# Strassen weight sums of an encoder's gated MLP: from accumulating DMAs into on-chip buffers, just in time, to batches in a DRAM scratch

## The reference, cut to what matters

```python
def conv_ffn(h, p, buf):
    u = h @ p['w_ffn_up']
    a, v = u[..., :D_FF], u[..., D_FF:]
    T = a.shape[1]
    ext = jnp.concatenate([buf.astype(a.dtype), a], axis=1)
    w = p['ffn_conv_w']
    c = p['ffn_conv_b'] + sum(ext[:, j:j + T] * w[j] for j in range(CONV_W))
    out = (jax.nn.silu(c) * v) @ p['w_ffn_down']
    return out, ext[:, -(CONV_W - 1):]

def layer(x, pos, p, lb, kv_past, pe_past, past_pos, S0, conv_buf, is_prompt):
    h = rmsnorm(x, p['norm_mix_pre'])
    mix, kv_lat, k_pe, S_new = token_mixers(h, pos, p, lb, kv_past, pe_past, past_pos, S0, is_prompt)
    x = x + rmsnorm(mix, p['norm_mix_post'])
    h = rmsnorm(x, p['norm_ffn_pre'])
    f, buf = conv_ffn(h, p, conv_buf)
    x = x + rmsnorm(f, p['norm_ffn_post'])
    return x, kv_lat, k_pe, S_new, buf
```

## Time and profile before

| | |
|---|---|
| three runs | 1931.81, 1934.43, 1935.34 us |
| profiled execution, its own time | 1932.28 us |
| its span | 1930.5 us |
| TensorE busy | 1820.8 us, 94% |
| VectorE, ScalarE, GpSimd busy | 1267.4, 951.0, 229.5 us |
| DMA moved | 204.03 MB, mean 106 GB/s |
| mean granted TensorE clock | 0.979 |

### The profile page before, as it was taken

One profiled execution on the slowest core, in us unless ns is written; L12 is line 12 of the kernel. 1 busy time (PEld: TensorE's weight loads), 2 busy tenths in 40 slices (PEclk: granted clock), 3 DMA queues, 4 the chain that ended last, 5 costly groups with the idle time before them and its releaser, 6 DMA issues.

```text
span 1930.5 us, 31256 instructions
## 1 busy us (share of the span) xinstructions
PE 1820.8 (94%) x11636; PEld 1668.9 (86%) x11636; DVE 1267.4 (66%) x1973; ACT 951.0 (49%) x1593; POOL 229.5 (12%) x257
## 2 busy tenths in 40 slices
PE   8999999999899999898799999999998999999985
PEld 7999975698899999898799999657988999999984
DVE  5777875526765665677767778653377665756776
ACT  5444546436653443535654444653466343535355
POOL 0000034100112121111000000340001111111100
PEclk9999999999999999999999999999999999999997
DMA  4312131411565665565131122323125565556621
GB/s 178 91 57 68 62 95 52 134 54 40 130 159 142 153 142 141 138 156 140 44 106 46 57 68 72 88 74 96 60 76 145 142 151 143 141 149 166 140 71 60
DMA packets 98902, 204.03 MB, mean 106 GB/s; under 512 B 16864, under 2 KB 35680, under 8 KB 98728
## 3 DMA queue, kind: packets, MB, share of 16 engines
q1 hardware_dynamic: 63952, 144.39, 23.5%
q0 software_dynamic: 21888, 39.86, 12.6%
q10 hardware_dynamic: 12912, 17.78, 2.8%
HBM read 170.98 MB, written 8.65 MB: 93 GB/s over the span
## 4 chain that ended last, share of the span: by engine, by line
PE 56%; DVE 17%; DMA 13%; ACT 9%; issue 3%; DVEq 0%; POOL 0%; ACTq 0%; SPq 0%; POOLq 0%
PE G L795 34%; PE WA L795 11%; PE WB L795 8%; DVE wlo L2158 5%; DMA t<-in_wstream 4%; DMA wraw<-in_wstream 2%; ACT whi L1480 2%; DMA t<-wraw 2%; DVE tmp L2158 2%; DMA wff<-in_wstream 2%; DVE cc L2158 1%; DMA wraw<-t 1%; DMA wff<-t 1%; PE G L799 1%; DVE ax L2158 1%
## 5 line engine op out<-in xcount | busy, mean ns | idle before, releaser
L795 PE MATMUL G<-Hh,wlo 128*128 128x328 f32 x1384 | 452.4, 327 | 11.8 <-DVE Hl L2158 8.0
L795 PE MATMUL G<-Hh,whi 128*128 128x328 f32 x1384 | 436.0, 315 | 0.0
L795 PE MATMUL G<-Hl,whi 128*128 128x328 f32 x1384 | 434.6, 314 | 0.0
L795 PEld LDWEIGHTS G<-Hh,wlo 128*128 128x128 f32 x1384 | 263.2, 190 | 23.3 <-DVE Hl L2158 12.1
L795 PEld LDWEIGHTS G<-Hh,whi 128*128 128x128 f32 x1384 | 263.4, 190 | 2.4 <-issue 0.6
L795 PEld LDWEIGHTS G<-Hl,whi 128*128 128x128 f32 x1384 | 263.1, 190 | 0.0
L1480 ACT ACTIVATE whi<-wraw 128x1024 fp32r<-128x1024 f32 (+2 forms) x171 | 155.6, 910 | 187.0 <-PE G L795 114.7
L2158 DVE TENSOR_TENSOR wlo<-wraw,whi 128x1024 fp32r<-128x1024 f32 (+2 forms) x171 | 177.6, 1038 | 54.4 <-ACT whi L1480 41.8
L795 PE MATMUL G<-gh,wlo 128*128 128x328 f32 x424 | 134.3, 317 | 10.1 <-DVE tmp L2158 9.3
L795 PE MATMUL G<-Sh,wlo 128*128 128x328 f32 x304 | 100.9, 332 | 34.2 <-ACT R L1480 34.2
L795 PE MATMUL G<-gh,whi 128*128 128x328 f32 x424 | 132.9, 313 | 0.0
(11 more groups left out here) (327 smaller groups left out, 4142.9 us busy)
## 6 DMA issues: line engine op xcount, KB each, us to landing
wraw<-in_wstream SPq DMA_DIRECT2D x108, 512.0 KB, 3.5
wff<-in_wstream SPq DMA_DIRECT2D x40, 512.0 KB, 4.6
t<-in_wstream SPq DMA_DIRECT2D x76, 256.0 KB, 4.4
t<-in_wstream POOLq DMA_DIRECT2D x38, 256.0 KB, 6.5
ckT<-in_ckT SPq DMA_DIRECT2D x12, 512.0 KB, 3.4
wff<-in_wstream POOLq DMA_DIRECT2D x20, 256.0 KB, 4.1
t<-wff POOLq DMA_DIRECT2D x20, 256.0 KB, 3.9
wff<-t POOLq DMA_DIRECT2D x20, 256.0 KB, 3.5
```

What stands on the lines that cost most here:

```text
L795: return pe.matmul(out, lhsT, rhs, start=start, stop=stop, skip_group_check=True)
```

## The change

1. The sums T1 to T4 no longer lie in on-chip buffers. A new internal DRAM tensor `wsum` (2 layers x 19 chunks x 128 x 2048 floats, as [T2 | T3 | T1 | T4]) holds them. POOL makes them in five batches of 4, 4, 3, 4 and 4 chunks a layer: three plain copies from `wstream` (u into the places of T1 and T4, B22 into T2, B12 into T3), then accumulating DMAs for T1 and T3, then T2, then T4, each step when the one before has landed.
2. In each layer POOL makes batches 0 and 1 (EARLY = 2) before the heads' work, in layer 0 after `tile` reached 4, and batches 2 to 4 after `split_out`, before the MLP.
3. SP loads four pieces for each chunk in place of two and two copies: u; [T2 | T3] and [T1 | T4] from `wsum`, and the right half of v (B22) with 256 KB.
4. `t2` and `t3` (3 halves) go, `wff` gets a third buffer: five raw buffers in all in the MLP.
5. LATE and PAIRS change: T1 and T4 are split as a pair, B22 alone.
6. DVE makes `g_low` of chunk 2 before the sums of activations and not behind them.

The changed lines, cut to their core:

```diff
-RAW, SPL = 2, 3
+RAW, SPL, SLOTS = 2, 3, 5
...
-LATE = {B11: 1, B21: 0, T2: 1, T3: 0, T1: 0, T4: 1, B22: 0}
-PAIRS = (B11, T2, T4)
+LATE = {B11: 1, B21: 0, T2: 1, T3: 0, T1: 1, T4: 0, B22: 0}
+PAIRS = (B11, T2, T1)
+CHUNK_PIECES = 4
+BATCHES = [(NPL, 7), (7, FH), (FH, 14), (14, 18), (18, KF)]
+EARLY = 2
...
+    wsum = nc.dram_tensor("wsum", [DEPTH, NS, P, 2 * W_PIECE], F32, kind="Internal").ap()
...
         def raw_slot(p):
-            return p % 2 if p < P_UP + 2 * NPL else p % 4
+            return p % RAW if p < P_UP + 2 * NPL else (p - P_UP) % SLOTS
...
+                    return [[(s, 0, W_PIECE, 0)], [(None, 0, W_PIECE, 0)], [(None, W_PIECE, 2 * W_PIECE, 0)],
+                            [(s + 1, W_HALF, W_PIECE, 0)]][p - p0]
...
                 for c, p0 in P_CHUNK.items():
                     if p == p0 + 1:
-                        sum_parts(l, c)
+                        name, n = summing(l, next(b for b, (c0, c1) in enumerate(BATCHES) if c0 <= c < c1))
+                        sp.wait_ge(S(name), n + 112)
...
+            def start_sums(l, b):
+                (u, v, t), (name, n) = stored_parts(l, b), summing(l, b)
+                if n:
+                    pool.wait_ge(S(name), n)
+                pool.dma_start(t[:, :, W_PIECE:2 * W_PIECE], u).then_inc(S(name), 16)
+                pool.dma_start(t[:, :, to_t2], v[:, :, right]).then_inc(S(name), 16)
+                pool.dma_start(t[:, :, to_t3], v[:, :, left]).then_inc(S(name), 16)
+            def sum_t1_t3(l, b):
+                (u, v, t), (name, n) = stored_parts(l, b), summing(l, b)
+                pool.wait_ge(S(name), n + 48)
+                pool.dma_start(t[:, :, to_t1], v[:, :, left], accum_op=ALU.add).then_inc(S(name), 16)
+                pool.dma_start(t[:, :, to_t3], v[:, :, right], accum_op=ALU.add).then_inc(S(name), 16)
+            def sum_t2(l, b):
+                t, (name, n) = stored_parts(l, b)[2], summing(l, b)
+                pool.wait_ge(S(name), n + 80)
+                pool.dma_start(t[:, :, to_t2], t[:, :, to_t1], accum_op=ALU.add).then_inc(S(name), 16)
+            def sum_t4(l, b):
+                t, (name, n) = stored_parts(l, b)[2], summing(l, b)
+                pool.wait_ge(S(name), n + 96)
+                pool.dma_start(t[:, :, to_t4], t[:, :, to_t2], accum_op=ALU.add).then_inc(S(name), 16)
+            def weight_sums(l, b0, b1):
+                for b in range(b0, b1):
+                    start_sums(l, b)
+                for b in range(b0, b1):
+                    sum_t1_t3(l, b)
+                for b in range(b0, b1):
+                    sum_t2(l, b)
+                for b in range(b0, b1):
+                    sum_t4(l, b)
+            pool.wait_ge(S("tile"), 4)
             for l in range(DEPTH):
+                weight_sums(l, 0, EARLY)
                 for h in range(HG):
...
                 split_out(l, range(HG))
-                sum_t1(l, NPL)
-                sum_t2(l, NPL)
-                for c in range(NPL, KF):
...
+                weight_sums(l, EARLY, len(BATCHES))
...
                         lows(l, u0 - 1)
+                        g_low(last_c)
...
-                    g_low(last_c)
+                    if q:
+                        g_low(last_c)
```

More of the change, by code:

```diff
@@ L86 @@
         U_PROD[_c], P_CHUNK[_c] = _u, _p
-        _u, _p = _u + PRODUCTS, _p + 2
+        _u, _p = _u + PRODUCTS, _p + CHUNK_PIECES
     U_PASS[_q], P_PASS[_q] = _u, _p
@@ L225, in build @@
         cout = sb(ff, "cout", [P, KF, 2 + DB * 2])
-        wff = sb(ff, "wff", [P, 2, W_PIECE])
-        t23 = sb(ff, "t23", [P, 3, W_HALF])
-        t2, t3 = t23[:, 0:2, :], t23[:, 2, :]
+        wff = sb(ff, "wff", [P, SLOTS - RAW, W_PIECE])
         tk = ExitStack()
@@ L257, in raw_slot @@
         def raw_slot(p):
-            return p % 2 if p < P_UP + 2 * NPL else p % 4
+            return p % RAW if p < P_UP + 2 * NPL else (p - P_UP) % SLOTS
         def raw_of(p):
-            return wraw[:, p % 2, :] if raw_slot(p) < 2 else wff[:, p % 2, :]
+            s = raw_slot(p)
+            return wraw[:, s, :] if s < RAW else wff[:, s - RAW, :]
         def last_unit(p):
             for c, p0 in P_CHUNK.items():
-                if p0 <= p < p0 + 2:
-                    return U_PROD[c] + (T4, B22)[p - p0]
+                if p0 <= p < p0 + CHUNK_PIECES:
+                    return U_PROD[c] + (B21, T3, T4, B22)[p - p0]
             return next((U_PASS[q] + p - p0 for q, p0 in P_PASS.items() if p0 <= p < p0 + GROUPS[q][1] - GROUPS[q][0]), p)
@@ L343, in raw_pair @@
             c, i = product_of(g % UNITS_L)
[L344 to L349, removed]
+            return raw_of(P_CHUNK[c] + i // 2).rearrange("p (a c) -> p a c", a=2)
         def raw_unit(g):
@@ L356, in raw_unit @@
             c, i = product_of(u)
[L357 to L360, removed]
+            return raw_of(P_CHUNK[c] + i // 2)[:, W_HALF * (i % 2):W_HALF * (i % 2) + W_HALF]
         def raw_ready(g):
@@ L367, in raw_ready, with summing @@
             c, i = product_of(u)
[L368 to L374, removed]
-            j = chunk_no(l, c)
-            return ("T3", 16 * (j + 1)) if i == T3 else ("T", 16 * (3 * j + {T1: 1, T2: 2, T4: 3}[i]))
+            return loaded[l * PIECES + P_CHUNK[c] + i // 2]
+        def summing(l, b):
+            n = l * len(BATCHES) + b
+            return f"sums{n % 3}", 112 * (n // 3)
         def act_took(l, c, i):
@@ L756, in sum_t4, with stored_parts @@
-            def sum_t4(l, c):
-                j, w = chunk_no(l, c), raw_of(P_CHUNK[c])
-                pool.wait_ge(S("w_split"), unit_of(j, B21) + 1)
-                sum_wait(l, c, T2)
-                pool.dma_start(w[:, W_HALF:W_PIECE], t2[:, j % 2, :], accum_op=ALU.add).then_inc(S("T"), 16)
+            def stored_parts(l, b):
+                c0, c1 = BATCHES[b]
+                s, n = S_UP[c0 // FH] + 2 * (c0 % FH), c1 - c0
+                return a["wstream"][l, s:s + 2 * n - 1:2], a["wstream"][l, s + 1:s + 2 * n:2], wsum[l, c0 - NPL:c1 - NPL]
@@ new lines, in _ @@
+            left, right = slice(0, W_HALF), slice(W_HALF, W_PIECE)
+            to_t2, to_t3, to_t1, to_t4 = (slice(W_HALF * i, W_HALF * i + W_HALF) for i in range(4))
+            def start_sums(l, b):
[5 more added lines that the diff above has]
+                pool.dma_start(t[:, :, to_t3], v[:, :, left]).then_inc(S(name), 16)
```

45 lines of the change are left out of this document (7 added, 38 removed).

## The result

The changed kernel takes 2018.58 us (median of 4 runs, 2014.65 to 2021.94) against 1934.56 us of the kernel before on the same chip: ratio 1.0436, 95% interval 1.0415 to 1.0458. It is 84 us slower where 14.7 us less was forecast. Two executions stand far apart and are counted in no number of this document: one of e11's four, at 4620.88 us, and one of the kernel before beside e12, at 2295.13 us.

A forecast was written before the change was run, and what follows sets the result against it. TensorE was busy 94% of the span, so time could come only from PE's waits or half clock. Terms -45.6 + 1.7 + 26.2 + 3 = -14.7 us gave a median of 1920 us, range 1889 to 1946.

The forecast's parts named there:

- The T2 waits: MLP products: PE's 34.2 us of waits for ACT's R and 15.4 us of low clock go; counted as -45.6 us.
- 4 us were kept back for the product T4: MLP products: 4 us of the gain held back for seven more 0.6 us waits of T4 for ACT's p.
- Split order and `g_low`: MLP: splitting T1, T4 ahead of R costs nothing; `g_low` ahead of the first down pass's sums costs +1.7 us.
- POOL's early batches: First head of layer 0: batches 0 and 1 delay POOL's first decay from 108.31 to 133 us; +26.2 us.
- the 1.7 us for the clock: First head of layer 0: half clock after PE's 24.5 us wait costs 1.7 us, part of the +26.2.
- adds at the second [rate] 38.4 us: Early batches of layer 0: their adds run at q0's 164 GB/s, the rate of adds alone, and take 38.4 us.
- The forecast's upper bound, 186 us: First head of layer 0: with copies at 164 GB/s and adds at half that, POOL is free at 186, 78 us late.
- The sample's attention: Late batches beside its key loads make one load late, 1.5 us a layer: +3 us, bounds 0 and 20.
- In the MLP stage ... nothing: MLP stage: copies of layer 1's first batches cost nothing, as SP's loads have 15 us for 3.5.
- Early batches of layer 1: They run behind layer 0's late ones, some 500 us before POOL's next decay: no cost.
- The slow sums: Rival, first head of layer 0: POOL free after 147 us, the MLP's gain used up, 1935 to 1973 us; chance 0.15.
- the hidden case: Rival, first head of layer 0: early sums hidden, POOL under 10 us late, 1892 to 1905 us; chance 0.28.

The follow-up runs named there:

- e11: The changed kernel with no sums made, SP loading stored weights in their place (wrong weights in five products of seven): 1897.46 us, ratio 0.9817 to the kernel before.
- e12: e10 with only batches 0 and 1 of layer 0 between the heads, all other batches at places in the MLP: 1899.24 us, ratio 0.9815 to the kernel before.
- e9: e7 with each late batch and each batch of layer 1 issued alone, at its own chunk of the MLP: 1909.51 us, ratio 0.9873 to the kernel before.
- e10: e9 with `g_low` of the first down pass back behind the sums of states: 1904.80 us, ratio 0.9846 to the kernel before.
- e1: The changed kernel with rows outermost in the adds of T1 and T3: 1971.48 us, ratio 1.0170 to the kernel before.
- e4: The changed kernel with each layer's late batches begun only when the sample's attention is done: 2010.95 us, ratio 1.0390 to the kernel before.
- e3: The changed kernel with the states loaded as 128 rows of 1408 B into a tile of their own: 1988.34 us, ratio 1.0261 to the kernel before.
- e2: e1 with rows outermost also in the three plain copies of a batch: 1961.57 us, ratio 1.0133 to the kernel before.
- e7: Changed kernel, e2's rows, e3's states; layer 0's batches 0 to 2 behind head decays, all others in the MLP products: 1918.87 us, ratio 0.9919 to the kernel before.

## Why the prediction was wrong

*The T2 waits: right, an eighth too large.* PE's waits for R went from 34.2 us to 0.8, those for ACT's p stayed at 5.7 us in 6, no `whi` waits for a DMA in the products, and 528 matmuls of them take 82.1 us (287.65 over 1850, times 528; 81 to 82 forecast). Of the 49.6 us at most, 40.4 came (the ledger's row, 21.9 and 18.5), where the sum has 45.6. Two sizes were off. The clock was counted as half of PE's busy time in the eight stretches, 15.4 us. PE's timeline of before shows what it costs; the first two rows are at the lower level, the others at the upper one:

```profile
717.26 0.48 PE L795 MATMUL G<-Sh,whi 128*128 128x328 f32 x1
717.53 0.48 PE L795 MATMUL G<-Sl,whi 128*128 128x328 f32 x1
...
719.27 0.31 PE L795 MATMUL WA<-Sh,wlo 128*128 128x328 f32 x1
719.42 0.31 PE L795 MATMUL WA<-Sh,whi 128*128 128x328 f32 x1
```

Matmuls start 273 ns apart there and 150 ns otherwise. Some 100 of them stand in the eight stretches, which is 12.3 us. (In the two product windows it is 90, or 11.1 us. PE's busy time fell by only 7.2 us there, since the first matmul after a gap is longer and there are more gaps now.) The other 6 us of what is missing went to short waits, where 4 us were kept back for the product T4: in the two product windows 36 starts come more than 0.3 us after the one before, where it was 27. The 5.1 us at the ends of the layers in e11 was no term of the sum; e12 does not have it.

*Split order and `g_low`: right.* No wait of PE shows the pair T1, T4 in the way (R is 0.8 us in all). The wait for Y is 5.9 us twice with the weights on time (e9, e11) against 5.8 forecast, and 4.9 with the step undone (e10), which is 2.5 us of the profile in both layers against 1.7 in the sum. In the changed kernel the wait was 4.3; its stage was held up by others.

*POOL's early batches: the step that failed first.* The mechanism, its place, and the price of 1 us for 1 us were right (51.7 us late, 51.4 us lost; the 1.7 us for the clock did not show); the decay came at 160.00 and not at 133. The step "adds at the second [rate] 38.4 us" took the rate of a queue whose DMAs had rows outermost for DMAs that have the batch outermost. With rows outermost the decay comes at 132.03 (e1). That this is within 1 us of the forecast is partly luck: both batches' copies went at 187 GB/s where the sum had q1's 318, though half hidden beside the first adds, and the steps behind the adds took 12.3 us (119.74 to 132.03) where the sum has some 20. The forecast's upper bound, 186 us, held it, but the reason named for it (a slow end in DRAM) was not the cause. That sentence should have asked for the shape of the new DMAs, which the diff shows.

*The sample's attention: too small.* +14.2 us against +3, inside the bound given (20 us for both layers). The term was reckoned for the key loads of 512 KB (6.8 us where they had 3.4). The loads of 64 KB suffered more, 7.6 us where they had 3.3, and they are on the path: PE waits for `cpe`, and in e4, without this traffic, no more.

*"In the MLP stage ... nothing": the step that failed outright*, and the largest. Of the ledger's 61.6 us there, 8.0 lie in the output projection and 2.1 stand in e11 too, without any sum; the rest, some 51 us, is the batches' traffic at the start of the MLP. The sentence looked at SP's weight loads in the products. But the late batches run into the start of the MLP, and there a load that was never in the list stands on the path: the states in 64 B pieces (34 of the 54 us, e3). And "*Early batches of layer 1* ... no cost" looked only at POOL's next decay: their copies run at the start of layer 0's MLP (from 561.57 us) beside its weight loads, and in e1 and e2 they alone keep layer 0's states late (ACT waits 19.9 and 26.5 us there, and for layer 1's not at all). With all batches out of that stage it costs nothing (e7). Within the products the claim holds for one batch at a time (e9; 2.0 us in e12), and not for three (e7).

Between the forecast and the profile lie 104 us (89.6 and 14.7): 60 in the row with the start of the MLP, 25 in the first head, 11 in the other heads and the sample's attention, 5 in the products, 3 at the ends of the layers.

*The rivals.* The slow sums won: POOL free after 147 us, but at 2019 and not up to 1973, because none of the rivals priced traffic beside the small loads. The time of the hidden case, 1892 to 1905, is reached at 1899 by e12, another kernel, with the batches elsewhere.

## What to carry to other kernels

Work that is moved off a stage onto the DMA engines is paid where the engines have no room: list every load that lands on the path while the new transfers run, small ones first, and give the transfers one place at a time in a stage with slack. Look at the outermost dimension of each new access pattern before taking a rate for it. A block on an engine's queue is spread only if each piece is shorter than the gap between the instructions that others wait for.

## What the runs showed of the hardware

- Adds with 4 chunks outermost moved 4.19 MB in 65 us, one alone at a DMA share of 0.28 and 52 GB/s, two at 0.57 and 104 GB/s; with the 128 rows outermost the same adds took 36 us (e1). q0 also had three times the packets (92768 against 30304 with all of them row by row in e2, for 80.13 and 79.70 MB); the extra ones carry 4 or 8 B.
- A load of 2816 pieces of 64 B lands in 4.0 us alone and in 30.8 us beside q0's 2 KB and 4 KB packets; as 128 rows of 1408 B it took 6.6 us beside them (e3) and 2.2 us alone (e7).
- Copies and adds from DRAM to DRAM took no more per packet than adds into on-chip buffers: q0's packets take 178 ns on average in e2 (17.2% of 16 times 1957.7 us over 30304 packets), as in the kernel before, beside whatever else was in flight.
- At the lower granted clock the matmuls of 328 columns started 273 ns apart, at the upper one 150 ns. The same last passes of layer 0 took 87.7 us in the kernel before, 87.8 in e12 and 90.9 in e11, the last at a mean granted clock of 0.94 and the others at 0.98.
